# Layer-norm gains on GpSimd, an earlier decay step and halved first loads in a hybrid encoder kernel

## The chip, the cores and the metric

The kernel runs on one core of a Trainium2 chip. The metric is the device time of one execution in microseconds (us); smaller is better. The kernel before took 1337.24 us, the median of 3 runs between 1337.15 and 1337.52. The core has five engines that run their own instruction streams and meet at semaphores: TensorE (PE, matmuls), VectorE (DVE), ScalarE (ACT), GpSimd (POOL) and SyncE (SP, which here only issues DMAs).

## The reference

Two sequences of 256 tokens and 1024 channels pass through an initial layer norm and then two layers. One layer, cut to what matters:

```python
proj = h @ w_in                          # q, k, v, z, xbc, dt side by side
attn_out = window_attention(rope(q), rope(k), v, sink)      # |i-j| <= 128, 8 heads, 2 kv heads
xbc = silu(depthwise_conv(xbc, ssd_conv_w, ssd_conv_b))     # width 5
y = bidir_ssd(xs, dt_raw, dt_bias, a_log, bm, cm) + ssd_d * xs
ssd_out = rms_norm(y * silu(z), ssd_norm_g)
mix = concatenate([attn_out, ssd_out]) @ w_out
h = layer_norm(ALPHA * h + mix, ln1_g, ln1_b)
gate, val = split(h @ w_up)
ffn = (silu(depthwise_conv(gate, w, b)) * val) @ w_down     # width 3
h = layer_norm(ALPHA * h + ffn, ln2_g, ln2_b)
```

`layer_norm` is `(x - mean) * rsqrt(var + eps) * g + b`. All inputs and both outputs are float32.

## The kernel before, in words

All 512 tokens are worked on together, as 4 blocks of 128 tokens (t = 0 to 3) or as 8 tiles of 128 channels. Each weight matrix is cut into units of 128x1024 values: 105 units for a layer, numbered 0 to 104. Unit 0 is dt, 1 to 6 are k, v and four of q, 7 to 18 the convolved channels, 19 to 26 z, 27 to 38 the output projection, 39 to 82 the MLP's up projection, 83 to 104 the down projection.

Precision is kept by splitting: every weight unit `raw` is rounded by ScalarE to `whi` (L542), and VectorE forms `wlo = raw - whi` (L1118, "the split of a unit"). Activations are split in the same way into a high and a low part. Each product is then three matmuls: high by high, high by low and low by high. Raw, high and low units lie in a ring of 5 slots; SP loads a unit when the unit five places ahead has been used, and the split of unit n + 4 is written into the steps of unit n.

The order of the mixer is one list, `SCHED`, made by `mixer_schedule()` (L91). Every engine walks the same list and issues its own part of each step. The steps that the change touches or that stand near it:

- `G` n: the matmuls of unit n. `E` n: ScalarE copies the unit's result out of PSUM. For q and k these are four copies into the single tile `ropet` (the swapped halves, L648) and one into `qk` (L651); the four wait for the rotation before.
- `ROT`: the rotation, three VectorE operations (L1353, L1355, L1356). `S` n: the high and low part of weight unit n.
- `AA`, `AO`, `SM` (at unit 5): cumulative decays for the state-space part. TensorE sums them, ScalarE copies the high parts (`own_hi` L679, `off_hi` L684), VectorE makes from them `own_z`, `off_z`, `cum_a`, `own_w` and `off_w` (L1318 to L1338).
- `F`, `F2`: the taps of the convolution (L1254), from unit 7 on. `AS`, `AM`, `AX`, `AD`, `AN`, `AP`, `AV`: the attention of one block, from unit 8 on; `AN` is GpSimd's scaling (L505), `AP` TensorE's transposes (L1058).
- `RMS` and `RN` (in the output projection): the reciprocal (L1432), then for each of the 8 channel tiles a product with the gain (L1433, L1441) and the low part `alo` (L1445). `GN` (L1435): two operations of `gain` each, in units 31 to 34.

`gain` (L1121) multiplies by the layer norm's gain row and then adds its shift row, in token layout, for the residual path: in `ha` for the first norm of a layer and in `hb` for the second, 8 operations of 128x1024 each. `ha` is loaded back from DRAM (`h_kept`, L456), where `hb` has been stored; the gain and shift rows `gb` are a DMA of 1 MB (L435). The semaphore `affined` counts these operations; the sums of the next layer norm wait for it.

Unit 27 + k of the output projection has its k-th input tile in `ahi`, `alo`. Tiles 0 to 3 are attention, 4 to 11 the normalized state-space output, so unit 31 waits for the first low part and for its own weight split. TensorE does the first three units in banks 0 to 5 early, and comes back to their banks 6 and 7 (6 matmuls each) once the `std` of RMS is read.

After the last layer, block t is finished by: the sum with the matmul result (L1138, for t = 3 in halves L1494), the mean, the centred product with the gain `y1` (L1501), on ScalarE the squares and the root (L547, L549), the reciprocal (L1162), and two halves of `hb = y1 * rstd + shift` (L1508), each stored by its own DMA.

## Time and profile before

The profiled execution took 1337.52 us; its span, from the first instruction to the last, is 1335.7 us.

| | busy us | share of the span | instructions |
|---|---|---|---|
| PE (matmul) | 1313.1 | 98% | 6692 |
| DVE | 801.7 | 60% | 1076 |
| ACT | 581.0 | 43% | 883 |
| POOL | 103.8 | 8% | 71 |

TensorE's mean granted clock was 0.998. Times in the rows below are counted from the span's start. A row of the timeline gives the start, the time taken in us, the engine, the source line, the operation, what it writes and reads by the program's names, the shapes, how many equal instructions were merged (x2), and in brackets how long the engine was idle before and which engine ended that. For merged instructions the time is that of all together. On TensorE matmuls overlap, so the distance between their starts counts and not their own duration.

### The profile page before, as it was taken

The numbers are of one execution on the slowest core, as the hardware profiler recorded it, in microseconds if no ns is written. First come the engines' busy times: TensorE is split into PE (matmuls) and PEld (weight loads), VectorE is DVE, ScalarE is ACT, GpSimd is POOL, SyncE is SP. The second block draws the span as 40 slices with busy tenths as digits, with TensorE's granted clock in tenths as the row PEclk, the third lists the DMA queues.
The fourth block names the chain that finished last, engine by engine and source line by source line (L and its number), as shares of the span: only waits on it lengthen the run. The fifth ranks groups of instructions, "written<-read, shape, count | busy, mean of one in ns | idle before, by whom it ended". The sixth has DMA issues, their size and how long they took to land.

```text
span 1335.7 us, 16322 instructions
## 1 busy us (share of the span) xinstructions
PE 1313.1 (98%) x6692; PEld 1078.9 (81%) x6692; DVE 801.7 (60%) x1076; ACT 581.0 (43%) x883; POOL 103.8 (8%) x71
## 2 busy tenths in 40 slices
PE   8999999999999999999999999999999999999997
PEld 7877777788888888888888777787788888888885
DVE  6787888867444444442367878788564444443425
ACT  5756554436333333311266665544363333333112
POOL 2013500001000000000020234000010000000000
PEclk9999999999999999999999999999999999999999
DMA  5421121423332323333234211224223333223332
GB/s 189 151 79 49 61 66 49 173 79 97 100 103 95 95 95 95 128 101 100 67 101 157 64 49 63 64 88 149 94 81 102 102 95 95 95 95 127 99 103 97
DMA packets 33786, 129.94 MB, mean 97 GB/s; under 512 B 3792, under 2 KB 3952, under 8 KB 32560
## 3 DMA queue, kind: packets, MB, share of 16 engines
q1 hardware_dynamic: 33552, 128.61, 29.3%
q8 instruction: 53, 0.87, 0.3%
q0 software_dynamic: 160, 0.29, 0.1%
q14 instruction: 21, 0.17, 0.0%
HBM read 122.59 MB, written 6.29 MB: 96 GB/s over the span
## 4 chain that ended last, share of the span: by engine, by line
PE 79%; DVE 10%; ACT 7%; issue 2%; DMA 1%; POOL 0%; SPq 0%; DVEq 0%; ACTq 0%; POOLq 0%
PE ps L782 16%; PE ps L784 16%; PE ps L783 16%; PE ps L832 8%; PE ps L834 8%; PE ps L833 8%; PE ps L1027 2%; ACT ropet L648 1%; DVE wlo L1118 1%; DMA raw<-in_units 1%; ACT junk L547 1%; ACT sc L714 1%; DVE hb L1138 1%; ACT whi L542 1%; PE ps L824 1%
## 5 line engine op out<-in xcount | busy, mean ns | idle before, releaser
L782 PE MATMUL ps<-hhi,whi 128*128 128x512 f32 (+1 forms) x1200 | 457.7, 381 | 2.3 <-DVE hlo L1185 2.3
L783 PE MATMUL ps<-hlo,whi 128*128 128x512 f32 (+1 forms) x1200 | 453.6, 378 | 0.0
L784 PE MATMUL ps<-hhi,wlo 128*128 128x512 f32 (+1 forms) x1200 | 453.5, 378 | 0.0
L1118 DVE TENSOR_TENSOR wlo<-raw,whi 128x1024 fp32r<-128x1024 f32 x210 | 262.9, 1255 | 167.4 <-ACT whi L542 167.4
L542 ACT ACTIVATE whi<-raw 128x1024 fp32r<-128x1024 f32 x210 | 221.2, 1056 | 220.5 <-DMA raw<-in_units 220.5
L782 PEld LDWEIGHTS ps<-hhi,whi 128*128 128x128 f32 x1200 | 225.7, 188 | 45.8 <-issue 2.8
L784 PEld LDWEIGHTS ps<-hhi,wlo 128*128 128x128 f32 x1200 | 225.7, 188 | 42.2
L783 PEld LDWEIGHTS ps<-hlo,whi 128*128 128x128 f32 x1200 | 225.9, 188 | 41.5
L832 PE MATMUL ps<-whi,uhi 128*128 128x512 f32 x352 | 137.1, 390 | 0.0
L833 PE MATMUL ps<-whi,ulo 128*128 128x512 f32 x352 | 137.0, 389 | 0.0
L834 PE MATMUL ps<-wlo,uhi 128*128 128x512 f32 x352 | 136.9, 389 | 0.0
L1456 DVE SCALAR_TENSOR_TENSOR gcv<-ps,pf,gcv 128x510 f32<-128x510 f32 x44 | 33.0, 749 | 154.7 <-ACT gcv L752 154.6
L752 ACT ACTIVATE gcv<-ps,pf 128x512 f32<-128x512 f32 x44 | 34.4, 781 | 169.3 <-PE ps L784 169.3
L1466 DVE TENSOR_TENSOR guf<-gsg,ps 128x512 f32<-128x512 f32 x44 | 30.3, 688 | 82.9 <-PE ps L784 82.3
L832 PE MATMUL ps<-whi,ahi 128*128 128x512 f32 x192 | 75.7, 394 | 1.7 <-ACT std L738 1.7
L834 PEld LDWEIGHTS ps<-wlo,uhi 128*128 128x128 f32 x352 | 66.1, 188 | 13.7
L833 PEld LDWEIGHTS ps<-whi,ulo 128*128 128x128 f32 x352 | 66.1, 188 | 13.7
L832 PEld LDWEIGHTS ps<-whi,uhi 128*128 128x128 f32 x352 | 66.1, 188 | 13.6
L834 PE MATMUL ps<-wlo,ahi 128*128 128x512 f32 x192 | 74.8, 389 | 0.0
L833 PE MATMUL ps<-whi,alo 128*128 128x512 f32 x192 | 74.8, 389 | 0.0
L1254 DVE SCALAR_TENSOR_TENSOR cv<-ps,pm,cv 128x508 f32<-128x508 f32 (+1 forms) x96 | 71.4, 744 | 3.8 <-ACT cv L638 1.2
L484 POOL TENSOR_TENSOR hlo<-hfm,hhi 128x512 fp32r<-128x512 f32 x16 | 21.1, 1334 | 664.5 <-ACT hhi L574 664.5
(169 smaller groups left out, 1332.0 us busy)
## 6 DMA issues: line engine op xcount, KB each, us to landing
raw<-in_units SPq DMA_DIRECT2D x210, 512.0 KB, 3.5
gb<-in_gb SPq DMA_DIRECT2D x5, 1024.0 KB, 5.7
h_kept<-hb SPq DMA_DIRECT2D x2, 2048.0 KB, 9.1
ha<-h_kept SPq DMA_DIRECT2D x2, 2048.0 KB, 8.3
hb<-in_x SPq DMA_DIRECT2D x4, 512.0 KB, 6.4
out_y<-hb SPq DMA_DIRECT2D x8, 256.0 KB, 2.0
cn<-in_cn SPq DMA_DIRECT2D x1, 583.5 KB, 10.0
pm<-in_pm POOLq DMA_DIRECT2D x2, 80.0 KB, 3.4
```

The costliest lines, as they stand in the source:

```text
L542: A(whi[:, m % RING, :], raw[:, m % RING, :], ACT.Copy).then_inc(unit_hi, 1)
L752: A(gcv[:], ps[:, bank, :], ACT.Identity, scale=pf[:, k * 3 + w0 + 1:k * 3 + w0 + 2], bias=pf[:, k + v0:k + v0 + 1]).then_inc(glu_center, 1)
L782: mm(out, whi[:, slot, cols], xhi, start=start, stop=False)
L783: mm(out, whi[:, slot, cols], xlo, start=False, stop=False)
L784: return mm(out, wlo[:, slot, cols], xhi, start=False, stop=stop)
L832: mm(ps[:, bank, :], xhi[:, rows], whi[:, slot, cols], start=start, stop=False)
L833: mm(ps[:, bank, :], xlo[:, rows], whi[:, slot, cols], start=False, stop=False)
L834: return mm(ps[:, bank, :], xhi[:, rows], wlo[:, slot, cols], start=False, stop=stop)
L1118: V.tensor_tensor(wlo[:, m % RING, :], raw[:, m % RING, :], f(whi[:, m % RING, :]), ALU.subtract).then_inc(unit_split, 1)
L1254: V.scalar_tensor_tensor(out=dst[:, :, lo:hi], in0=src[:, :, lo + s:hi + s], scalar=pmc("conv_w", 5 * j + tap, 5 * j + tap + 1), in1=dst[: ...
L1456: V.scalar_tensor_tensor(out=dst[:, :, 1:SEQ], in0=src[:, :, 0:SEQ - 1], scalar=pf[:, k * 3 + w0:k * 3 + w0 + 1], in1=dst[:, :, 1:SEQ], op ...
L1466: V.tensor_tensor(guf[:], gsg[:], ps[:, bank + 1, :], ALU.mult).then_inc(glu_done, 1)
```

## The change

Five things are changed. (1) `AA`, `AO`, `SM` stand ahead of unit 5's rotation and weight split instead of behind them. (2) All `gain` operations go from VectorE to GpSimd, in a new function `affine` that does the four products and then the four additions. (3) The first two blocks of x are loaded in halves with a semaphore for each, and the statistics of the first half wait only for it. (4) For the last norm, `y1` has two buffers; for blocks 0 and 1, ScalarE multiplies by `rstd` and GpSimd adds the shift row, and one DMA stores each of these blocks. (5) The order of SP's last stores follows.

```diff
@@ mixer_schedule
+        if n == 5:
+            steps += [("AA", 0), ("AO", 0), ("SM", 0)]
         if n - 1 == U_V:
             steps += [("VT", 0)]
...
         steps += [("F", n)]
-        if n == 5:
-            steps += [("AA", 0), ("AO", 0), ("SM", 0)]
...
         steps.append(("S", u + AHEAD))
-        i = u - U_OUT - 4
-        if 0 <= i < NBLK:
-            steps += [("GN", 2 * i), ("GN", 2 * i + 1)]
@@ SP
             for t in range(2):
-                sp_eng.dma_start(hb[:, t, :], x_in[t]).then_inc(x_loaded[t], 16)
+                for half in range(2):
+                    cols = slice(half * 512, (half + 1) * 512)
+                    sp_eng.dma_start(hb[:, t, cols], x_in[t][:, cols]).then_inc((x_left if half == 0 else x_loaded)[t], 16)
...
-            for t in range(NBLK):
+            for t in range(2):
+                sp_eng.wait_ge(y_shifted, t + 1)
+                sp_eng.dma_start(y_d[t], hb[:, t, :]).then_inc(y_stored, 16)
+            for t in range(2, NBLK):
                 for half in range(2):
                     cols = slice(half * 512, (half + 1) * 512)
-                    sp_eng.wait_ge(y_ready, 2 * t + half + 1)
+                    sp_eng.wait_ge(y_ready, 2 * (t - 2) + half + 1)
                     sp_eng.dma_start(y_d[t][:, cols], hb[:, t, cols]).then_inc(y_stored, 16)
@@ GpSimd
+            def affine(idx, h):
+
+                pool.wait_ge(gb_loaded, idx * 16 + 16)
+                for t in range(NBLK):
+                    nc.gpsimd.tensor_tensor(h[:, t, :], h[:, t, :], gb[:, 0, :], ALU.mult).then_inc(affined, 1)
+                for t in range(NBLK):
+                    pool.wait_ge(affined, idx * 2 * NBLK + t + 1)
+                    nc.gpsimd.tensor_tensor(h[:, t, :], h[:, t, :], gb[:, 1, :], ALU.add).then_inc(affined, 1)
...
+                pool.wait_ge(h_loaded, L * 16 + 16)
+                affine(2 * L, ha)
                 lows(2 * L + 1)
+                pool.wait_ge(tp_full, (2 * L + 2) * NBLK)
+                affine(2 * L + 1, hb)
                 if L < DEPTH - 1:
                     lows(2 * L + 2)
+            pool.wait_ge(gb_loaded, (NORMS - 1) * 16 + 16)
+            for t in range(2):
+                pool.wait_ge(y_normed, t + 1)
+                nc.gpsimd.tensor_tensor(hb[:, t, :], hb[:, t, :], gb[:, 1, :], ALU.add).then_inc(y_shifted, 1)
@@ ScalarE
                     for t in range(NBLK):
-                        squares(2 * L + 2, t)
+                        squares(idx, t)
+                        if t < 2:
+                            act.wait_ge(ln_rstd, idx * NBLK + t + 1)
+                            act.wait_ge(y_scaled, t + 1)
+                            A(hb[:, t, :], y1[t][:], ACT.Copy, scale=st[:, t, 3:4]).then_inc(y_normed, 1)
@@ VectorE
-                dve.wait_ge(x_loaded[t], 16)
                 for half in range(2):
+                    dve.wait_ge((x_left if half == 0 and t < 2 else x_loaded)[t], 16)
...
-                    elif what == "GN":
-                        if i == 0:
-                            dve.wait_ge(h_loaded, L * 16 + 16)
-                        gain(2 * L, ha, i)
...
-                    if i == 0:
-                        dve.wait_ge(tp_full, (2 * L + 2) * NBLK)
-                    if 0 <= i < 2 * NBLK:
-                        gain(2 * L + 1, hb, i)
...
                     rstd(idx, t)
+                    if t < 2:
+                        continue
```

What this does to the order of the instructions, at three places. First, VectorE at units 4 to 6 of a layer, before (`ropet`, `qk` are a rotation, `wlo` a weight split, `own_z` to `off_w` the step SM):

```order
L1118 TENSOR_TENSOR wlo<-raw,whi 128x1024
L1353 TENSOR_TENSOR ropet<-ropet,cn 128x512
L1355 TENSOR_TENSOR qk<-qk,cn 128x512
L1356 TENSOR_TENSOR qk<-qk,ropet 128x512
L1118 TENSOR_TENSOR wlo<-raw,whi 128x1024
L1318 SCALAR_TENSOR_TENSOR own_z<-own_hi,cn,ps 128x512
L1324 SCALAR_TENSOR_TENSOR off_z<-off_hi,cn,ps 64x256 x2
L1328 TENSOR_SCALAR cum_a<-own_z,cn 128x512
L1330 TENSOR_SCALAR own_w<-own_z,cn 128x512 x2
L1338 TENSOR_SCALAR off_w<-off_z,cn 64x2x128 x4
L1353 TENSOR_TENSOR ropet<-ropet,cn 128x512
```

The same place now, from the split of unit 8 on (line numbers are those of the changed kernel):

```order
L1144 TENSOR_TENSOR wlo<-raw,whi 128x1024
L1335 SCALAR_TENSOR_TENSOR own_z<-own_hi,cn,ps 128x512
L1341 SCALAR_TENSOR_TENSOR off_z<-off_hi,cn,ps 64x256 x2
L1345 TENSOR_SCALAR cum_a<-own_z,cn 128x512
L1347 TENSOR_SCALAR own_w<-own_z,cn 128x512 x2
L1355 TENSOR_SCALAR off_w<-off_z,cn 64x2x128 x4
L1370 TENSOR_TENSOR ropet<-ropet,cn 128x512
L1372 TENSOR_TENSOR qk<-qk,cn 128x512
L1373 TENSOR_TENSOR qk<-qk,ropet 128x512
L1144 TENSOR_TENSOR wlo<-raw,whi 128x1024
L1370 TENSOR_TENSOR ropet<-ropet,cn 128x512
```

The five rows of SM have gone in front of one rotation and one weight split. Second, GpSimd from the last heads products to the next layer's start, before (`hlo` are low parts for the two layer norms, four each):

```order
L525 TENSOR_TENSOR heads_81<-cum_a,cn 128x1024
L514 TENSOR_TENSOR x_d_77<-xsc,pm 128x512 x3
L484 TENSOR_TENSOR hlo<-hfm,hhi 128x2x256 x8
L493 DMA pm<-in_pm 128x160
L494 DMA pf<-in_pf 128x120
```

The same place now:

```order
L538 TENSOR_TENSOR heads_81<-cum_a,cn 128x1024
L527 TENSOR_TENSOR x_d_77<-xsc,pm 128x512 x3
L495 TENSOR_TENSOR ha<-ha,gb 128x1024 x4
L498 TENSOR_TENSOR ha<-ha,gb 128x1024 x4
L488 TENSOR_TENSOR hlo<-hfm,hhi 128x2x256 x4
L495 TENSOR_TENSOR hb<-hb,gb 128x1024 x4
L498 TENSOR_TENSOR hb<-hb,gb 128x1024 x4
L488 TENSOR_TENSOR hlo<-hfm,hhi 128x2x256 x4
L506 DMA pm<-in_pm 128x160
L507 DMA pf<-in_pf 128x120
```

Eight operations on `ha` and eight on `hb` have come in, and each group of low parts stands behind one. Third, ScalarE at the end of the program, before (`junk` are the squares of one block):

```order
L547 ACTIVATE junk,st<-hb,st 128x1024
L549 ACTIVATE st<-st,cn 128x1
L547 ACTIVATE junk,st<-hb,st 128x1024
L549 ACTIVATE st<-st,cn 128x1
L547 ACTIVATE junk,st<-hb,st 128x1024
```

The same place now:

```order
L568 ACTIVATE junk,st<-hb,st 128x1024
L570 ACTIVATE st<-st,cn 128x1
L799 ACTIVATE hb<-y_0_97,st 128x1024
L568 ACTIVATE junk,st<-hb,st 128x1024
L570 ACTIVATE st<-st,cn 128x1
L799 ACTIVATE hb<-y_1_98,st 128x1024
L568 ACTIVATE junk,st<-hb,st 128x1024
```

A product with `rstd` stands behind the squares of blocks 0 and 1.

## Rows read from the trace of the kernel before

**Rows 1.** The page's first part: busy us (share) xinstructions of each engine.
```profile
PE 1313.1 (98%) x6692; PEld 1078.9 (81%) x6692; DVE 801.7 (60%) x1076; ACT 581.0 (43%) x883; POOL 103.8 (8%) x71
```
**Rows 2.** TensorE's waits: line, released by, us in total, times, longest us.
```profile
PE ps L824 <- DVE hb L1157: 2.4, 2, 1.3
```
**Rows 3.** Timeline of TensorE, 56 to 83 us.
```profile
56.99 0.50 PE L782 MATMUL ps<-hhi,whi 128*128 128x512 f32 x1
...
68.01 0.39 PE L782 MATMUL ps<-hhi,whi 128*128 128x512 f32 x1
...
73.45 0.39 PE L1042 MATMUL ps<-cut,big_i 128*128 128x256 f32 x2
...
82.16 1.09 PE L1058 MATMUL ps<-cn,sc 128*128 128x128 f32 x8 [0.28 <-POOL sc L505]
```
**Rows 4.** Timeline of ScalarE, the same stretch.
```profile
59.54 1.05 ACT L542 ACTIVATE whi<-raw 128x1024 fp32r<-128x1024 f32 x1
60.49 0.59 ACT L679 ACTIVATE own_hi<-ps 128x512 fp32r<-128x512 f32 x1
...
62.77 2.44 ACT L648 ACTIVATE ropet<-ps 32x512 f32<-32x512 f32 x4 [1.03 <-PE ps L784]
65.23 0.60 ACT L651 ACTIVATE qk<-ps 128x512 f32<-128x512 f32 x1
```
**Rows 5.** Timeline of VectorE, the same stretch.
```profile
62.25 0.74 DVE L1318 SCALAR_TENSOR_TENSOR own_z<-own_hi,cn,ps 128x512 fp32r<-128x512 f32 x1
...
66.85 0.69 DVE L1353 TENSOR_TENSOR ropet<-ropet,cn 128x512 f32<-128x512 f32 x1
...
70.16 3.16 DVE L1254 SCALAR_TENSOR_TENSOR cv<-ps,pm,cv 128x508 f32<-128x508 f32 x4
```
**Rows 6.** Timeline of GpSimd, 145 to 152 us.
```profile
145.28 4.21 POOL L525 TENSOR_TENSOR heads<-cum_a,cn 128x1024 fp32r<-128x1024 f32 x2
```
**Rows 7.** Timeline of VectorE, the same stretch.
```profile
145.84 1.89 DVE L1261 SCALAR_TENSOR_TENSOR xsc<-xsc,cv 128x512 f32<-128x512 f32 x1 [0.40 <-ACT xsc L669]
147.65 2.92 DVE L1118 TENSOR_TENSOR wlo<-raw,whi 128x1024 fp32r<-128x1024 f32 x1
```
**Rows 8.** The page's costliest groups: count, busy us, mean ns, idle before.
```profile
L484 POOL TENSOR_TENSOR hlo<-hfm,hhi 128x512 fp32r<-128x512 f32 x16 | 21.1, 1334 | 664.5 <-ACT hhi L574 664.5
```
**Rows 9.** Timeline of VectorE, 250 to 262 us.
```profile
251.27 3.35 DVE L1432 RECIPROCAL std<-std 128x512 f32<-128x512 f32 x1 [3.84 <-ACT std L738]
...
257.99 1.22 DVE L1118 TENSOR_TENSOR wlo<-raw,whi 128x1024 fp32r<-128x1024 f32 x1
```
**Rows 10.** Timeline of TensorE, the same stretch.
```profile
251.38 0.47 PE L832 MATMUL ps<-whi,ahi 128*128 128x512 f32 x1 [0.87 <-ACT std L738]
```
**Rows 11.** Timeline of SyncE's DMA queue, 240 to 262 us.
```profile
242.49 0.33 SPq L456 DMA_DIRECT2D ha<-h_kept  x1
```
**Rows 12.** Line L456, the loads of ha of both layers.
```profile
DMA to landing us min/median/max: 7.9/8.3/8.7
```
**Rows 13.** Timeline from 0 to 32 us, the warm-up matmuls.
```profile
1.00 6.25 PE L796 MATMUL ps<-avg 128*128 128x128 f32 x36 [1.00 <-POOL avg L487]
...
10.18 2.40 PE L796 MATMUL ps<-avg 128*128 128x128 f32 x20
```
**Rows 14.** Timeline of VectorE, 1314 to 1336 us.
```profile
1314.72 1.22 DVE L1138 SCALAR_TENSOR_TENSOR hb<-hb,ps 128x1024 f32<-128x1024 f32 x1 [9.14 <-PE ps L834]
...
1316.17 1.29 DVE L1501 SCALAR_TENSOR_TENSOR y<-hb,st,gb 128x1024 f32<-128x1024 f32 x1
...
1317.78 0.17 DVE L1162 RECIPROCAL st<-st 128x1 f32<-128x1 f32 x1 [0.32 <-ACT st L549]
...
1328.47 0.68 DVE L1494 SCALAR_TENSOR_TENSOR hb<-hb,ps 128x512 f32<-128x512 f32 x1
```
**Rows 15.** Timeline of TensorE, 1324 to 1336 us.
```profile
1326.47 0.39 PE L834 MATMUL ps<-wlo,uhi 128*128 128x512 f32 x1
```
**Rows 16.** The chain of waits, 0 to 14 us: start us, us, what.
```profile
2.12 6.65 DMA raw<-in_units
```

More of the change, by code:

```diff
@@ L268, in trunk @@
         junk = at("junk", 102, [P, D_MODEL])
-        y1 = at("y1", 88, [P, D_MODEL])
+        y1 = [at("y1_0", 88, [P, D_MODEL]), at("y1_1", -CT * TOK * 4 // KB, [P, D_MODEL], start=base_h)]
         std = at("std", 92, [P, TOK])
@@ L294, in trunk @@
         x_loaded = [sem(f"x_loaded{t}") for t in range(NBLK)]
+        x_left = [sem(f"x_left{t}") for t in range(2)]
         pm_loaded, pf_loaded = sem("pm_loaded"), sem("pf_loaded")
@@ L327, in trunk @@
         h_low, h_lows = sem("h_low"), sem("h_lows")
+        y_normed, y_shifted = sem("y_normed"), sem("y_shifted")
         glu_center, glu_taps, glu_silu = sem("glu_center"), sem("glu_taps"), sem("glu_silu")
@@ L468, in _ @@
             load_gb(NORMS - 1)
-            for t in range(NBLK):
+            for t in range(2):
+                sp_eng.wait_ge(y_shifted, t + 1)
+                sp_eng.dma_start(y_d[t], hb[:, t, :]).then_inc(y_stored, 16)
+            for t in range(2, NBLK):
                 for half in range(2):
                     cols = slice(half * 512, (half + 1) * 512)
-                    sp_eng.wait_ge(y_ready, 2 * t + half + 1)
+                    sp_eng.wait_ge(y_ready, 2 * (t - 2) + half + 1)
                     sp_eng.dma_start(y_d[t][:, cols], hb[:, t, cols]).then_inc(y_stored, 16)
-            sp_eng.wait_ge(y_stored, NBLK * 2 * 16)
+            sp_eng.wait_ge(y_stored, 6 * 16)
         @block.gpsimd
@@ L771, in _ @@
                 else:
+                    idx = 2 * L + 2
                     for t in range(NBLK):
-                        squares(2 * L + 2, t)
+                        squares(idx, t)
[3 more added lines that the diff above has]
+                            A(hb[:, t, :], y1[t][:], ACT.Copy, scale=st[:, t, 3:4]).then_inc(y_normed, 1)
         @block.tensor
@@ L1119, in split @@
                                     ALU.subtract).then_inc(unit_split, 1)
-            def gain(idx, h, i):
-                t, row = i % NBLK, i // NBLK
-                if i == 0:
-                    dve.wait_ge(gb_loaded, idx * 16 + 16)
-                if row:
-                    dve.wait_ge(affined, idx * 2 * NBLK + t + 1)
-                V.tensor_tensor(h[:, t, :], h[:, t, :], gb[:, row, :], ALU.add if row else ALU.mult).then_inc(affined, 1)
             def sums(idx, t, last_unit=0):
@@ L1474, in _ @@
                     split(unit(L, n + AHEAD))
-                    i = n - U_DOWN - 3
-                    if i == 0:
-                        dve.wait_ge(tp_full, (2 * L + 2) * NBLK)
-                    if 0 <= i < 2 * NBLK:
-                        gain(2 * L + 1, hb, i)
                 if L < DEPTH - 1:
@@ L1500, in _ @@
                     dve.wait_ge(ln_mu, (idx - 1) * NBLK + t + 1)
-                    V.scalar_tensor_tensor(out=y1[:], in0=hb[:, t, :], scalar=st[:, t, 1:2], in1=gb[:, 0, :],
+                    V.scalar_tensor_tensor(out=y1[t % 2][:], in0=hb[:, t, :], scalar=st[:, t, 1:2], in1=gb[:, 0, :],
                                            op0=ALU.add, op1=ALU.mult).then_inc(y_scaled, 1)
                     rstd(idx, t)
+                    if t < 2:
+                        continue
                     dve.wait_ge(ln_rstd, idx * NBLK + t + 1)
@@ L1507, in _ @@
                         cols = slice(half * 512, (half + 1) * 512)
-                        V.scalar_tensor_tensor(out=hb[:, t, cols], in0=y1[:, cols], scalar=st[:, t, 3:4], in1=gb[:, 1, cols],
+                        V.scalar_tensor_tensor(out=hb[:, t, cols], in0=y1[t % 2][:, cols], scalar=st[:, t, 3:4], in1=gb[:, 1, cols],
                                                op0=ALU.mult, op1=ALU.add).then_inc(y_ready, 1)
```

## The prediction

> **What bounds the kernel now.** I read the page's first part, then TensorE's waits, then the timeline of each engine where the change touches it. TensorE is busy for 98% of the span [rows 1]; its idle time is the start, the end and waits of about a microsecond, such as 2.4 us in two waits for the first normalized block [rows 2]. So work taken off VectorE in mid-kernel buys nothing unless TensorE waits for VectorE there, and a stall put on TensorE in mid-kernel comes back in full, for nothing later has room to absorb it. The questions are two: can the change shorten the ends, and does it make TensorE wait in the middle?
>
> **The block decay step moved ahead (SM at unit 5), in both layers.** TensorE's order stays; ScalarE and VectorE change. In the first layer unit 8's matmuls start at 68.01 and reuse the bank of unit 6, which ScalarE has copied out by 65.83 (65.23 + 0.60) [rows 3, 4]. After the change own_hi goes where the weight split stood, at 59.54, and ends at 60.1 [rows 4]. VectorE then runs SM, 66.85 - 62.25 = 4.6 us [rows 5], until 64.7, and only then the rotation of unit 5, three operations of 0.69, 2.1 us, until 66.8. ScalarE's copies of unit 6 wait for that rotation, because they write the one ropet tile: they take 2.44 + 0.60 [rows 4] and end at 69.9. TensorE's unit 8 so starts 1.9 us late. VectorE's next rotation waits for the swapped rows at 69.3, ends at 71.4, the split behind it (1.22 [rows 9]) at 72.6, and the convolution taps start at 72.7 instead of 70.16 [rows 5]: 2.5 us late. From there the chain taps, score maximum, exponentials, GpSimd scaling ends in the transposes at 82.16, where TensorE already waits 0.28 us for GpSimd [rows 3], so the whole 2.5 us arrive at TensorE (the 1.9 are inside them). Before, this ran under TensorE's matmuls because unit 6's copies overlapped SM; that cover is what the move takes away. Bounds: 1.9 if the chain has 0.6 us of slack that I don't see, 3.5 if ScalarE's table load falls badly. I take 2.5, twice: **+5.0 us**. The nearest ground for "nothing" would be slack at unit 8, but the copy ends only 2.2 us ahead of it and slips by 4.1.
>
> **The gains (GN and those in the down projection) moved from VectorE to GpSimd.** 16 operations per layer of 128x1024, both inputs in SBUF. GpSimd's price: its 128x512 subtraction with two SBUF inputs takes 1.33 us on average [rows 8], its broadcast product of 128x1024 takes 4.21 us for two, of which I show below that VectorE held up a part, so about 1.8 each [rows 6]. Bounds for one: 1.8 and 2 x 1.33 = 2.7; I take 2.5, near twice the dense one.
> The hb gains start when gb has landed in the down projection, where VectorE has nothing but one split per unit with three units in hand; eight take 20 us and nobody is waiting: 0.
> The ha gains are different. GpSimd starts when h_kept is back: issued at 242.49 [rows 11], landing 8.7 us later in this layer [rows 12], at 251.2. That is exactly when VectorE begins the reciprocal (251.27) and behind it, back to back, the norm products and low parts, all with two SBUF inputs, and the split of unit 31 at 257.99 [rows 9].
> What the trace shows of two such operations at once: GpSimd runs two heads products from 145.28, 4.21 us in all [rows 6]. VectorE's product xsc<-xsc,cv begins at 145.84 and lasts 1.89 us; the split behind it begins at 147.65 and lasts 2.92 us instead of 1.22 [rows 7, 9]. So the first waited for GpSimd's first product to end (147.1), then GpSimd's second went ahead of the split, which waited for 149.4. They take turns, and each waits for the other's whole instruction.
> The Trainium skill, "SBUF — State Buffer", section "Who interferes with whom", says the same of a VectorE instruction with two SBUF inputs against a GpSimd one that reads SBUF: the one that starts first blocks the other fully. It spares VectorE instructions with an input from PSUM, such as the taps; by that rule the loss sits in the norm stage and not in the convolutions. It says nothing of who is next, which I read from the turns above.
> Turn by turn: GpSimd's products 1 and 2 until 256.2; norm product 0 (due at 254.6); then one GpSimd operation ahead of each of product 1, low 0, product 2, low 1 and the split of unit 31. That makes 7 GpSimd operations and 5 VectorE ones of (257.99 - 254.62)/5 = 0.67, where 254.62 is the reciprocal's end, 251.27 + 3.35 [rows 9]: 251.2 + 7 x 2.5 + 5 x 0.67 + 1.2 = 273.3. TensorE needs that split for unit 31. It has 18 + 24 matmuls before it from 251.38 [rows 10], at (73.45 - 56.99)/72 = 0.229 each [rows 3]: 261.0. Stall: 12.3 us. The next split follows after the eighth GpSimd operation and four short ones, at 273.3 + 2.5 + 2.7 + 1.2 = 279.7, when TensorE has finished unit 31 at 278.8: 0.9 more. From there VectorE is alone and ahead again. Together 13.2 us. In the second layer the load takes 7.9 us [rows 12] and the same sum gives 0.9 less, 12.3. **+25.5 us.**
> A silent TensorE may come back slower. At the program's start, out of idleness, the warm-up matmuls take 6.25 us for 36 passes; ten microseconds later the same take 2.40 us for 20 [rows 13]. At the later pace of 0.12 the first ones would have taken 4.3, so they lost 1.9 us. The mean granted clock of the run is 0.998, so no fall in mid-kernel is shown. Per stall that is between 0 and 1.9 us, and 0.9 of it hides in the second wait; I take the slow start at its full size less that, 1.0 each, **+2.0 us**.
> The Trainium skill, "TensorE: Matmul & The Clock Gate", section "Why this matters for your kernels", warns of such gaps in the middle of a kernel: the clock falls to 1.2 GHz. No run here shows it yet; without it the sum is 2.0 less.
>
> **The end.** VectorE paces it: TensorE's last matmul starts at 1326.47 [rows 15], and VectorE gets to block 3 only at 1328.47 [rows 14], since each block costs it (1328.47 - 1314.72)/3 = 4.58 us against TensorE's 18 matmuls, 4.1. A block's y product starts 1.45 us after its sum. Blocks 0 and 1 lose their last VectorE step, some 1.4 us (two halves of the y product's kind, 1.29 for the whole). Alone that lets VectorE start block 2 at 1322.9 when it is ready, and block 3 at 1327.5: -1.0. But GpSimd's additions (hb and gb, 2.5 us) get in the way of the y products (hb and gb too). Block 0: reciprocal at 1317.78, ScalarE's product 1.1 (its rounding of the same shape takes 1.05 [rows 4]), addition 1319.1 to 1321.6. Block 1 is ready at 1318.8, its y is due at 1320.25 and waits to 1321.6, ends at 1322.9; its addition runs 1324.2 to 1326.7; block 2's y is due at 1324.55, waits to 1326.7, and the rest of block 2 ends at 1329.55. Block 3 starts there: **+1.1 us**. Bounds -1.0 and +1.3.
>
> **The start.** The chain is the load of unit 0 (issued 2.12, landed 8.77) and then ScalarE's rounding and VectorE's split [rows 16]. The x blocks arrive before that; halves give a sooner first statistic that nobody waits for. Two more issues on the queue put unit 0's issue 0.9 us back, but the engines are still full with x then. Between 0 and +0.9; I take **+0.2**.
>
> **Sum.** 5.0 + 25.5 + 2.0 + 1.1 + 0.2 = 33.8 on the profiled execution's 1337.5: 1371.3. That execution lies 0.3 above the median, so 1371.0 us.
>
> **Rivals.**
> 1. VectorE keeps the ports once it has them, and GpSimd gets in only where VectorE pauses. Then norm product 0 waits 1.5 us and the split of unit 31 is ready at 260.7, just ahead of TensorE. For it: only two turns of this kind are in the trace, one per layer. Against it: in both GpSimd's second product went ahead of a waiting split. It gives 1337.2 + 5.0 + 1.1 + 0.2 = 1343.5.
> 2. Turns are taken, but GpSimd loses every second one (its dispatch is slow against 0.67 us steps), or its operation costs 1.8. With 5 instead of 7 the stall is 5 us shorter in each layer: about 1359. With 1.8 us it is 7 x 0.7 = 4.9 shorter: the same 1359. Nothing in the trace speaks for the first; the row of 4.21 us for two speaks a little for the second.
> 3. The other side: faster. VectorE's inputs in the norm stage and the end don't collide with GpSimd's, and SM's move has slack. Place: the end, -1.0 us, deciding from the point where GpSimd's additions no longer hold the y products. 1336.2. Against it are the two stretched rows of VectorE [rows 7].
> 4. The change has no effect at all because TensorE never waits for what moved: 1337.
>
> **Chances.** Forecast (full turns) 0.65; rival 2, 0.16; rival 1, 0.13; rival 3 and 4 together 0.06. The forecast's own range: GpSimd's operation at 2.3 to 2.7 (-2.8 to +2.8 over both layers), clock 0 to 1.9 each, SM 1.9 to 3.5, ends: 1364 to 1379. The range for 8 in 10 reaches to rival 2: 1355 to 1380. A measurement of this kernel tells 0.2% (2.7 us) from no change. Faster by more than that 0.02, within it 0.04, slower 0.94.
>
> **What would show it.** In the profile after: VectorE's norm products, low parts and the split of unit 31 each lengthened to about 3 us just after the reciprocal, alternating with GpSimd's eight gains; TensorE idle for 11 to 13 us in front of unit 31 in both layers, put down to the split; the first matmuls behind it perhaps at twice their spacing. In units 6 to 9, a wait of about 2 us in front of unit 8 for ScalarE's qk copy. At the end, the y products of blocks 1 and 2 at about 2.6 us or more, and block 3 begun about 3 us after TensorE's last matmul. The prediction is wrong if the splits in the norm stage keep 1.2 us, or if TensorE doesn't stop before unit 31.

## The result, and the profile after

The changed kernel takes 1368.19 us in the median of 4 runs (1366.8 to 1370.16), the kernel before 1337.2 us on the same chip: ratio 1.0232, 95% interval 1.0215 to 1.025. The forecast was 1371.0. The profiled execution's span grew by 31.3 us, from 1335.7 to 1367.0, while TensorE's instructions stayed 6692 and VectorE's fell by 36.

TensorE's waits in the profile after (total, number, longest):

```profile
PE ps L858 <- DVE wlo L1144: 18.8, 2, 9.9
PE ps L850 <- DVE hb L1174: 3.0, 2, 1.7
PE ps L808 <- ACT qk L672: 2.2, 2, 1.9
```

The first row is new: two waits for a weight split. The second was already there [rows 2]; the third is the wait ahead of unit 8. To see where 31.3 us arose I compared the start of the same TensorE instruction in both traces:

| place | before | after | shift |
|---|---|---|---|
| first matmul of unit 0 | 13.67 | 14.20 | +0.5 |
| first attention block, layer 1 | 73.45 | 77.79 | +4.3 |
| after the convolutions | 110.70 | 114.24 | +3.5 |
| end of layer 1's mixer | 299.73 | 315.69 | +16.0 |
| small matmuls of the decays, layer 2 | 699.68 | 717.52 | +17.8 |
| first transposes, layer 2 | 739.11 | 757.89 | +18.8 |
| end of layer 2's mixer | 956.72 | 987.48 | +30.8 |
| VectorE's block 3 at the end | 1328.47 | 1359.78 | +31.3 |

So there are two steps of 12.4 and 12.0 us, one in each layer's norm stage; 3.0 and 2.8 us in the early units; and half a microsecond each at the start and at the end. In layer 2, 1.7 of the 2.8 us arise before unit 8, where TensorE ran at half clock for some 3 us behind a wait that stands in the kernel before too (1.05 us here, 0.99 before, where the clock held). The last section comes back to this.

VectorE in the norm stage of layer 1, after (start, duration, operation, idle time before):

```profile
254.86 3.35 DVE L1449 RECIPROCAL std<-std 128x512 f32<-128x512 f32 x1 [3.84 <-ACT std L759]
258.25 2.01 DVE L1450 SCALAR_TENSOR_TENSOR zs<-zs,pm,std 128x512 f32<-128x512 f32 x1
260.18 2.88 DVE L1454 SCALAR_TENSOR_TENSOR zs<-zs,pm,std 128x512 f32<-128x512 f32 x1
...
268.54 2.83 DVE L1458 TENSOR_TENSOR alo<-zs,ahi 128x512 fp32r<-128x512 f32 x1
271.29 3.36 DVE L1144 TENSOR_TENSOR wlo<-raw,whi 128x1024 fp32r<-128x1024 f32 x1
274.57 2.85 DVE L1454 SCALAR_TENSOR_TENSOR zs<-zs,pm,std 128x512 f32<-128x512 f32 x1
277.34 0.68 DVE L1458 TENSOR_TENSOR alo<-zs,ahi 128x512 fp32r<-128x512 f32 x1
```

GpSimd beside it:

```profile
254.96 10.36 POOL L495 TENSOR_TENSOR ha<-ha,gb 128x1024 f32<-128x1024 f32 x4 [79.62 <-DMA ha<-h_kept]
265.27 11.59 POOL L498 TENSOR_TENSOR ha<-ha,gb 128x1024 f32<-128x1024 f32 x4
```

And TensorE, where a matmul follows the last by 0.227 us at full clock:

```profile
264.38 0.39 PE L860 MATMUL ps<-wlo,ahi 128*128 128x512 f32 x1
274.70 0.80 PE L858 MATMUL ps<-whi,ahi 128*128 128x512 f32 x1 [9.93 <-DVE wlo L1144]
275.29 0.63 PE L859 MATMUL ps<-whi,alo 128*128 128x512 f32 x1
...
279.13 0.44 PE L859 MATMUL ps<-whi,alo 128*128 128x512 f32 x1
279.42 0.39 PE L860 MATMUL ps<-wlo,ahi 128*128 128x512 f32 x1
```

Before, the reciprocal was followed by steps of 0.67 us and the split of unit 31 at 257.99 [rows 9]. Now every step of VectorE from the second product on grows by about 2.13 us for as long as GpSimd has gains to run (until 276.86), and falls back to 0.68 at once afterwards. The first product meets GpSimd in the middle of an instruction and grows by 1.26. The split is ready at 274.65, and TensorE goes on at 274.70. The reciprocal keeps its 3.35 us, although GpSimd runs beside it. Behind the wait the matmuls start 0.43 us apart until 279.1, half the normal pace; the granted clock of these stretches:

```profile
274.00:276.00 2.00, 1.30 (x3) 1.11 (x4) 2.00 (x2) 0.00 (x0) 2.00 (x1) 0.50 0.00 0
...
280.00:282.00 2.00, 2.00 (x11) 1.63 (x10) 2.00 (x4) 0.88 (x2) 0.00 (x0) 1.00 0.00 0
```

The third number from the right is the clock: 0.50 (1.2 GHz), later 1.00 (2.4 GHz). Layer 2 shows the same, with a wait of 8.82 us and slow matmuls from 945.76 to 951.5.

### The profile page after: what moved, and what is told of

Read it like the earlier page. It is cut to its first block, busy times and chain, and to the rows that moved or that the text cites. A ratio compares the mean times of both kernels' runs of the same rounds, so it can differ in the third digit from the quotient of the medians.

```text
span 1367.0 us, 16323 instructions
## 1 busy us (share of the span) xinstructions
PE 1322.9 (97%) x6692; PEld 1084.7 (79%) x6692; DVE 800.5 (59%) x1040; ACT 583.5 (43%) x885; POOL 197.1 (14%) x105
## 4 chain that ended last, share of the span: by engine, by line
PE 79%; DVE 11%; ACT 7%; issue 1%; DMA 1%; POOL 0%; SPq 0%; DVEq 0%; ACTq 0%; POOLq 0%
PE ps L808 16%; PE ps L809 16%; PE ps L810 16%; PE ps L858 7%; PE ps L859 7%; PE ps L860 7%; PE ps L1053 2%; ACT ropet L669 1%; DVE wlo L1144 1%; ACT sc L735 1%; PE ps L850 1%; DVE hb L1155 1%; ACT junk L568 1%; DVE ast L1419 1%; DMA raw<-in_units 1%
## 5 line engine op out<-in xcount | busy, mean ns | idle before, releaser
L1144 DVE TENSOR_TENSOR wlo<-raw,whi 128x1024 fp32r<-128x1024 f32 x210 | 274.1, 1309 | 193.9 <-ACT whi L563 193.9
L858 PE MATMUL ps<-whi,ahi 128*128 128x512 f32 x192 | 78.3, 408 | 20.5 <-DVE wlo L1144 18.8
L495 POOL TENSOR_TENSOR hb<-hb,gb 128x1024 f32<-128x1024 f32 x8 | 22.0, 2776 | 498.2 <-DMA gb<-in_gb 498.2
```

The source lines that it names most:

```text
L858: mm(ps[:, bank, :], xhi[:, rows], whi[:, slot, cols], start=start, stop=False)
L1144: V.tensor_tensor(wlo[:, m % RING, :], raw[:, m % RING, :], f(whi[:, m % RING, :]), ALU.subtract).then_inc(unit_split, 1)
```

## The experiments

Each of the moved parts alone, then changed in the way that separates two causes. "Before" was run beside each; its median lay between 1337.4 and 1337.9.

### The ha gains alone

```
-        if 0 <= i < NBLK:
-            steps += [("GN", 2 * i), ("GN", 2 * i + 1)]
+                pool.wait_ge(h_loaded, L * 16 + 16)
+                affine(2 * L, ha)          # GpSimd, ahead of lows
```

> Only the gains and shifts of ha are moved to GpSimd; everything else is the kernel before. Theory (turns: while GpSimd has a two-input operation to run, each of VectorE's operations of 0.67 us waits for GpSimd's whole one and the next waits again, 2.8 us a pair): the split of unit 31 is ready at about 273.3 to 274.7 instead of before TensorE needs it at 261, in both layers, so 24 us longer: 1361.5 (1359 to 1363.5), with VectorE's rows at 2.8 us in both norm stages and TensorE idle 9 to 10 us on that split. Rival (the move of these operations costs little and the time comes from the moved decay step and the tail together with it): at most 1341. Rival (VectorE goes at its own pace and is only delayed once by 2.5): 1341 to 1343.

Measured: 1361.2 us in the median of 4 runs, ratio 1.0171 (1.0152 to 1.019). One of the four took 2670 us, for a reason that no trace shows; the others took 1360.0 to 1361.7, median 1360.65, which is +23.3. VectorE's steps take 2.87 and 2.88 us there, and

```profile
PE ps L840 <- DVE wlo L1126: 18.8, 2, 9.9
```

is the same row as in the whole change. This one part makes 23 to 24 of the 31 us. In its trace 0.9 of the 24.2 us that it is longer come from half clock at the start of layer 2.

### The same gains, a few microseconds later

```
                 pool.wait_ge(h_loaded, L * 16 + 16)
+                pool.wait_ge(sl_done, L * CT + CT)
                 affine(2 * L, ha)
```

> As the one with only the ha gains on GpSimd, but GpSimd also waits until VectorE has made the last of the eight low parts of the normalized output, so the same sixteen... (eight) operations run a few us later, beside a TensorE that has its weights split ahead. Theory turns: what costs is only that the operations meet the one stretch in which VectorE is late for TensorE; here VectorE has slack of several us, so the same operations cost 0 to 2 us: 1337.2 (1336.5 to 1339.5), though VectorE's operations beside them are still stretched to 2.8 us in the rows. Rival (GpSimd's operations cost TensorE's time by themselves, by memory traffic, or the whole stage waits for ha): it stays at 1355 or above.

Measured: 1337.86 us (10 runs), ratio 1.0004 (0.9995 to 1.0013). The collision is still in the trace, VectorE first, then GpSimd:

```profile
268.35 16.72 DVE L1127 TENSOR_TENSOR wlo<-raw,whi 128x1024 fp32r<-128x1024 f32 x5 [0.25 <-ACT whi L551]
```

```profile
268.23 12.43 POOL L488 TENSOR_TENSOR ha<-ha,gb 128x1024 f32<-128x1024 f32 x4 [96.98 <-DVE alo L1454]
```

Five splits take 16.72 us, 3.34 each instead of 1.22, but TensorE spends 24 matmuls of 0.227, 5.4 us, on a unit and has no wait between 267 and 290 us. The same eight operations per layer cost 23 to 24 us or, within the interval, at most 1.7, depending on whether TensorE is waiting for VectorE's work when they run. A cost of that size by GpSimd or its memory traffic as such is ruled out.

### The gains in halves

```
-                    nc.gpsimd.tensor_tensor(h[:, t, :], h[:, t, :], gb[:, 0, :], ALU.mult)
+                        for half in range(2):
+                            cols = slice(half * 512, (half + 1) * 512)
+                            ins = nc.gpsimd.tensor_tensor(h[:, t, cols], h[:, t, cols], gb[:, row, cols], ...)
```

> As the one with only the ha gains on GpSimd, but as 16 operations of 128x512 per layer instead of 8 of 128x1024. Theory turns (VectorE waits for one whole instruction of GpSimd before each of its own): each of VectorE's operations in the norm stage is stretched by about 1.1 to 1.3 instead of 2.13 us (rows of 1.8 to 2.0 for those that take 0.68 to 0.75), the eight rows ahead of TensorE's need end at about 265.5 instead of 273.3, so TensorE's first wait is 2 to 3 us instead of 9.9 and then further ones come while GpSimd still runs: each unit then needs one split and four operations, (1.22 + 4 x 0.72 + 5 x 1.2) = 10 against 3.6 us of TensorE, so the rest of the delay comes back as later waits: in all 18 to 24 us over both layers, 1355 to 1361. Rival (the total of GpSimd's busy time beside VectorE decides, as a shared bandwidth): each operation stretched by a fixed factor of about 4 as before, first wait unchanged at 9.9, 1361. Rival (shorter instructions let VectorE pass): 1345 or less.

Measured: 1354.84 us (1354.2 to 1355.7), ratio 1.0125 (1.0111 to 1.0139), just below my range. VectorE in the norm stage:

```profile
257.58 1.78 DVE L1457 TENSOR_TENSOR alo<-zs,ahi 128x512 fp32r<-128x512 f32 x1
259.29 1.77 DVE L1453 SCALAR_TENSOR_TENSOR zs<-zs,pm,std 128x512 f32<-128x512 f32 x1
260.98 1.75 DVE L1457 TENSOR_TENSOR alo<-zs,ahi 128x512 fp32r<-128x512 f32 x1
262.66 2.28 DVE L1130 TENSOR_TENSOR wlo<-raw,whi 128x1024 fp32r<-128x1024 f32 x1
```

With GpSimd's instruction half as long, what is added to each VectorE step is half as long: 1.77 - 0.72 = 1.05 us instead of 2.13. A shared bandwidth would have left the factor of 4 alone. TensorE's waits in front of unit 31 and the two units behind it are 3.66, 0.39 and 1.09 us in layer 1 (I had expected 2 to 3 for the first), and 4.10 and 1.67 in layer 2. The work gets through sooner although GpSimd does the same amount: per turn VectorE does a step for 1.05 us of GpSimd and not for 2.13.

### GpSimd only writes

```
+                for n in range(40):
+                    nc.gpsimd.memset(scratch[:], 0.0).then_inc(filled, 1)
+                    pool.wait_ge(filled, L * 40 + n + 1)
```

> The kernel before, with 40 memsets of 128x512 on GpSimd beside the norm stage of each layer, at the time at which the moved ha gains would run; they write to an unused piece of SBUF and nothing reads it. What the two engines contend for: theory A (the path by which both read two operands, so a GpSimd instruction that only writes doesn't hold VectorE): VectorE's rows stay 0.68 and 0.75, 1337.4 (1336.8 to 1338). Theory B (any GpSimd instruction that touches SBUF takes its turn with VectorE): rows of VectorE grow by the length of one memset (0.3 to 0.6 us) each, TensorE waits for the split of unit 31 a few us or not at all, 1338 to 1350.

Measured: 1337.4 us (10 runs), ratio 0.9998 (0.9989 to 1.0007). GpSimd, then VectorE inside that stretch:

```profile
250.43 23.36 POOL L533 MEMSET scratch<- 128x512 f32 x40 [79.17 <-DMA ha<-h_kept]
```

```profile
256.90 0.68 DVE L1451 TENSOR_TENSOR alo<-zs,ahi 128x512 fp32r<-128x512 f32 x1
257.50 1.22 DVE L1124 TENSOR_TENSOR wlo<-raw,whi 128x1024 fp32r<-128x1024 f32 x1
```

Forty memsets back to back leave VectorE's rows where they were. So GpSimd's writing to SBUF doesn't hold VectorE. By elimination what collides is its reading of operands (theory A); a GpSimd instruction that reads only one was not tried, so this step is argued and not shown. The other half of the condition stands in the changed kernel's own trace, in an attention block: VectorE's taps read one operand from PSUM, and beside GpSimd's two-operand scaling

```profile
83.51 1.52 DVE L1271 SCALAR_TENSOR_TENSOR cv<-ps,pm,cv 128x510 f32<-128x510 f32 x2
```

```profile
83.74 1.89 POOL L518 TENSOR_TENSOR sc<-sc,ast 128x1024 f32<-128x1024 f32 x1 [54.02 <-DVE ast L1430]
```

neither is stretched: the two taps take 1.52 us, as the pair at 81.04 does (1.53) with GpSimd idle. The scaling takes 1.89, its mean over all 16.

### The hb gains alone

```
+                pool.wait_ge(tp_full, (2 * L + 2) * NBLK)
+                affine(2 * L + 1, hb)      # GpSimd; VectorE's gain() calls go
```

> Only the gains and shifts of hb are moved to GpSimd, which runs them beside VectorE's splits of the down projection. Theory turns: VectorE's splits beside them go from 1.22 to 3.35 us, which is less than the 3.63 us that TensorE takes for a unit, and they are made units ahead, so TensorE never waits for one: 1337.4 (1337.0 to 1338.2). Rival (any meeting of the two engines costs TensorE time in proportion to the overlap, 2 x 8 x 2.1 us): 1350 or more. Rival (VectorE is relieved of 16 operations of 1.2 us and the end of the layer comes earlier): 1336.5 or less.

Measured: 1337.63 us (11 runs), ratio 0.9998 (0.9989 to 1.0006). No cost is seen, and one above 0.8 us is ruled out. The splits beside the gains take 1.65 to 2.63 us, less than I expected, since VectorE idles over 3 us before each and meets only part of a GpSimd instruction. (A unit is 24 matmuls, 5.4 us, and not the 3.63 of the expectation; that makes the slack larger.)

### The decay step alone

```
+        if n == 5:
+            steps += [("AA", 0), ("AO", 0), ("SM", 0)]     # ahead of the splits
         ...
-        if n == 5:
-            steps += [("AA", 0), ("AO", 0), ("SM", 0)]     # was behind F
```

> Only the step of the decay sums (AA, AO, SM at unit 5) is moved ahead of the splits. Theory: in each layer ScalarE copies ropet and qk 1.9 us late, unit 8 and the first attention block start 1.9 to 2.5 us late, and in layer 1 the wait of 1.9 us is followed by some 3 us at half clock (1.6 us more). From the two traces: +3.0 in layer 1 and +0.9 in layer 2, so 1341.2 (1339.5 to 1343). Rival of the prediction as written (2.5 in each layer, reaching the transposes, plus the clock): 1342.2 to 1344. Rival (the step costs nothing by itself and the 3 us are an after-effect of the later start): 1337.2 to 1338.

Measured: 1342.83 us (1342.4 to 1343.3), ratio 1.004 (1.0026 to 1.0054), +5.4. The wait ahead of unit 8, and the matmuls behind it:

```profile
69.67 0.50 PE L782 MATMUL ps<-hhi,whi 128*128 128x512 f32 x1 [1.89 <-ACT qk L651]
70.02 0.55 PE L783 MATMUL ps<-hlo,whi 128*128 128x512 f32 x1
...
73.35 0.48 PE L782 MATMUL ps<-hhi,whi 128*128 128x512 f32 x1
73.66 0.39 PE L783 MATMUL ps<-hlo,whi 128*128 128x512 f32 x1
```

Behind a wait of 1.9 us come 3 us at half pace (a later run shows the same wait without them). My account (3.0 in layer 1 because of the clock, 0.9 in layer 2) came to 1.5 us too little; the time lies in the range of the prediction as written. Layer 2 cost 2.7: its first 1.7 are a fall of the clock at its start, which the 1.0 of the later stage only tops up. That asks whether the clock is a cost at all, and the next two runs test it.

### Matmuls without use in front of unit 8, and then also at the start of layer 2

```
                         if i == 8:
+                            keep_warm(8, 5)
...
                     elif what == "DTT":
+                        if L:
+                            keep_warm(4, 5)       # second of the two kernels only
```

> The moved decay step alone, and eight matmuls without use (0.24 us each) on TensorE just ahead of its wait for unit 8, in both layers. Theory (the 1.9 us wait itself remains, but the 1.6 us that the half clock takes behind it in layer 1 goes): 1342.8 - 1.6 = 1341.2 (1340.4 to 1342), PEclk 1.00 from 66 to 78 us. In layer 2 the wait there is only 0.3 us, so the eight matmuls (1.9 us) would hold unit 8 up by some 1.6 us unless the next stage has slack: then 1342.8 and the gain of layer 1 is eaten. Rival (the clock falls for another reason than the wait): the same rows of 0.63 us at 70 to 74 us, 1342.8 or more.

> As the kernel with the moved decay step and the matmuls before unit 8, and four more matmuls without use (1.0 us) ahead of TensorE's wait for the copy of zt at the start of layer 2 (a wait of 1.0 to 1.15 us in every run, behind which the clock fell in five profiles and not in five others). Theory (filling that wait keeps the clock whole, 1.65 us in a profile that had the fall): 1.0 to 1.7 us less than the kernel with only the first eight matmuls, PEclk 1.00 from 688 to 700 us. Rival (the fall there is not brought on by the wait): no difference between the two, within 0.3 us.

Measured: 1342.73 us (1342.4 to 1343.0) and 1342.43 us (1342.3 to 1342.7). Both are within 0.4 of the decay step alone: my expectation of 1.6 less, and of another 1.0 to 1.7 less, failed. (The 1342.8 that I gave for a second outcome was met, but not for its reason: in layer 2 the eight matmuls did put unit 8 back, by 1.4 us, and at the end of the convolutions only 0.2 of it was left.) Yet the clock did what I asked. From 70 to 74 us, first the decay step alone, then with the eight matmuls:

```profile
70.00:74.00 4.00, 4.00 (x12) 3.15 (x11) 3.79 (x6) 3.46 (x4) 0.00 (x0) 0.57 0.16 65
```

```profile
70.00:74.00 4.00, 3.95 (x17) 3.30 (x18) 3.87 (x6) 3.84 (x4) 0.00 (x0) 1.00 0.18 74
```

The clock is 1.00 instead of 0.57, and the first attention block starts at 75.60 instead of 76.87. It buys next to nothing, because TensorE then stands in front of the first transposes:

```profile
84.70 1.09 PE L1060 MATMUL ps<-cn,sc 128*128 128x128 f32 x8 [0.68 <-POOL sc L505]
```

Before that wait was 0.28 [rows 3]; in the decay step alone it is gone in this layer, and so is a later one of 0.60 for `alo`. The late chain through ScalarE, VectorE and GpSimd sets these places, and whether TensorE comes to them early or late matters little. Counted from unit 0, the layer ends 2.6 us late with the clock held and 3.0 without: the fall of 1.6 us costs 0.4. At the start of layer 2 it is the same. In the second of the two kernels the clock holds there (1.00 from 690 to 694, against 0.65 in the first), layer 2's first stage is 1.7 us shorter, and the wait at the transposes (743.99, 0.67 us for GpSimd) is still there: the decay step now costs 2.65 in that layer instead of 1.0.

### The halved loads of x alone

```
-                sp_eng.dma_start(hb[:, t, :], x_in[t]).then_inc(x_loaded[t], 16)
+                for half in range(2):
+                    cols = slice(half * 512, (half + 1) * 512)
+                    sp_eng.dma_start(hb[:, t, cols], x_in[t][:, cols])...
```

> Only the loads of the first two blocks of x are made in halves (four DMAs of 256 KB instead of two of 512 KB). Theory (the second half of block 1 lands last, at 7.5 us instead of the whole block before it, and the statistics of block 1 and so the first unit start 0.5 us later): first unit's matmuls at 14.2 instead of 13.7, 1337.9 (1337.4 to 1338.6). Rival of the prediction (two more issues of 0.05 us each, +0.2): 1337.4 to 1337.6. Rival (the first half is there earlier and the start gains): 1336.8 or less.

Measured: 1338.52 us (11 runs) against 1337.9, ratio 1.0003 (0.9994 to 1.0012): too small for the times. The trace has unit 0 at 14.38 instead of 13.67, +0.7. Unit 0 starts at 13.14 to 13.82 in the eleven profiles with whole loads and at 14.00, 14.20 and 14.38 in the three with halves, so some 0.7 us are lost there. In the changed kernel the chain to unit 0 runs through block 1 of x:

```profile
6.55 0.69 DVE L1166 BATCH_NORM_STATS2 moms<-hb 128x6 f32<-128x512 f32 x1 [1.37 <-DMA hb<-in_x]
7.56 0.69 DVE L1166 BATCH_NORM_STATS2 moms<-hb 128x6 f32<-128x512 f32 x1 [0.31 <-DMA hb<-in_x]
```

The statistics of block 1 wait for its second half, and its transposes end at 11.45. With the loads alone changed, the chain that sets unit 0 runs through its load, as before (start, us, what):

```profile
3.06 6.42 DMA raw<-in_units
```

It is issued at 3.06 instead of 2.12, because each of the two further issues takes 0.42 us with 0.05 between them (the expectation counts the 0.05 alone), and lands at 9.48 instead of 8.77: 0.71 later, what unit 0 loses. The two chains lie within 0.3 us of each other in both traces. The profile is 1.5 us longer in all; 0.9 of it are half clock at the start of layer 2, behind a wait of 1.07 us.

### The end alone

```
+                        if t < 2:
+                            A(hb[:, t, :], y1[t][:], ACT.Copy, scale=st[:, t, 3:4]).then_inc(y_normed, 1)
...
+            for t in range(2):
+                pool.wait_ge(y_normed, t + 1)
+                nc.gpsimd.tensor_tensor(hb[:, t, :], hb[:, t, :], gb[:, 1, :], ALU.add).then_inc(y_shifted, 1)
```

> Only the end is changed: for blocks 0 and 1 the last operation of the final layer norm goes to ScalarE (scaling) and GpSimd (shift). Theory (the two y operations of VectorE at the end wait for GpSimd's shift, 1.3 to 2.6 and 3.3 us, which eats what two fewer pairs of VectorE operations save): +0.5 against before, 1337.7 (1337.2 to 1338.3). Rival (VectorE is freed of 2 x 1.3 us and the end comes earlier): 1336.2. Rival (a second cost, ScalarE's reading of y1, comes on top): 1339 or more.

Measured: 1338.06 us (11 runs), ratio 1.0005 (0.9996 to 1.0014). The gain of 1 us is ruled out; +0.7 or nothing can't be told apart. In the trace two `y` products wait for GpSimd's addition:

```profile
1319.57 2.56 DVE L1514 SCALAR_TENSOR_TENSOR y<-hb,st,gb 128x1024 f32<-128x1024 f32 x1
...
1323.65 3.30 DVE L1514 SCALAR_TENSOR_TENSOR y<-hb,st,gb 128x1024 f32<-128x1024 f32 x1
```

They took 1.28 before. The 3.3 us given away eat up the two pairs of VectorE operations saved, 2 x 1.42. VectorE comes to block 3 2.54 us after TensorE's last matmul starts (1325.85), and 2.00 us in the kernel before: +0.5.

### The whole change, with the ha gains late

The edit is the one line of the second experiment, put into the changed kernel.

> The changed kernel with one thing more: GpSimd waits for the last of the eight low parts of the normalized output before the ha gains. Theory (the sum of the parts measured alone: decay step +5.4, x loads +0.6, hb 0, end +0.7, ha late +0.5): 1337.4 + 7.2 = 1344.6 (1343 to 1346.5), so the whole of the other 24 us is the meeting of the ha gains with the norm stage. Rival (parts that cost nothing alone cost something together, such as the hb gains against a VectorE that is already late): 1348 or more. Rival (the gains of the other parts show only now): 1341 or less.

Measured: 1344.87 us (1344.7 to 1345.0), ratio 1.0052 (1.0036 to 1.0067). One wait takes 23.3 of the 31 us back, and the parts add up: 1337.4 + 5.4 + 0.6 + 0 + 0.7 + 0.5 = 1344.6 (the last four terms are each too small to be told from nothing by themselves). The trace shows one thing more, in layer 1 in front of unit 8:

```profile
70.41 0.50 PE L809 MATMUL ps<-hhi,whi 128*128 128x512 f32 x1 [1.91 <-ACT qk L673]
70.75 0.40 PE L810 MATMUL ps<-hlo,whi 128*128 128x512 f32 x1
70.98 0.39 PE L811 MATMUL ps<-hhi,wlo 128*128 128x512 f32 x1
```

The same wait of 1.91 us as in the changed kernel, and the clock holds (1.00 from 70 to 76). Behind the wait of 1.92 us in layer 2 (730.24) it falls. Counted from unit 0, layer 1's early units cost 2.6 us here, as with the matmuls without use.

### The end in another order, on the kernel before

```
                     y1[t % 2] = (hb - mean) * gain        # block t
+                    if t:
+                        shifted(t - 1, 1)                  # second half of block t - 1
                     rstd(idx, t)
                     ...
                     shifted(t, 0)
```

> The kernel before with another order of VectorE's work at the very end: the second half of block t-1's last operation stands behind the centred product of block t, so that it fills the wait for the root on ScalarE. Theory (each of the three blocks before the last then hides one operation of about 0.75 us, but only the last blocks' queue counts, since VectorE waits for TensorE's block 3): -0.8 us, 1336.6 (1336.2 to 1337.1). Rival (VectorE waits for block 3's matmuls at the end anyway, so the order before them is worth nothing): 1337.4, within 0.3.

Measured: 1336.34 us (11 runs), ratio 0.9988 (0.9979 to 0.9996): faster than the kernel before, by 1.6 in the medians and 1.2 in the spans, where I had expected 0.8. VectorE:

```profile
1320.07 1.28 DVE L1507 SCALAR_TENSOR_TENSOR y<-hb,st,gb 128x1024 f32<-128x1024 f32 x1
1321.27 0.75 DVE L1488 SCALAR_TENSOR_TENSOR hb<-y,st,gb 128x512 f32<-128x512 f32 x1
1321.93 0.16 DVE L1162 RECIPROCAL st<-st 128x1 f32<-128x1 f32 x1
...
1326.97 0.68 DVE L1500 SCALAR_TENSOR_TENSOR hb<-hb,ps 128x512 f32<-128x512 f32 x1
```

The wait of 0.32 us for the root [rows 14] is filled in blocks 1, 2 and 3, and block 3 starts at 1326.97 instead of 1328.47. Moving VectorE's work within VectorE got what moving it to GpSimd did not.

## Why the prediction was right

**The turns (forecast +25.5).** The mechanism is as read from [rows 6, 7, 9]: seven GpSimd instructions run before VectorE's split of unit 31 does, and one stands ahead of every VectorE step. The whole-instruction wait was tested (halves) and holds: a turn is one whole GpSimd instruction and the VectorE step behind it. That writing alone doesn't collide (memsets) and that an operand from PSUM spares VectorE (taps) are in the traces. The size was off: a GpSimd gain adds 2.13 us to a turn, where I took 2.5 from the nearest rows. That is outside my range of 2.3 to 2.7, and a little nearer to the 1.8 of rival 2 than to my 2.5. Seven times 0.37 is 2.6 us per layer, and TensorE's waits are 9.9 and 8.8 instead of 12.3 and 11.4. The second wait of 0.9 did not come, since TensorE was slow just then. Waits together: 18.8 against 25.5. The Trainium skill, "SBUF — State Buffer", section "Who interferes with whom", spares a VectorE instruction with an operand from PSUM; the taps agree, at 0.76 us each beside GpSimd. That the engines alternate, instruction by instruction, is read from the row of every turn.

**The slow clock behind the waits (forecast +2.0).** This was too small. The step at layer 1 is 12.4 - 9.9 = 2.5 us beyond the wait, at layer 2 12.0 - 8.8 = 3.2: together 5.7, of which the half pace makes 2.2 and 2.9. I had read the loss from the program's start, 1.9 us at most [rows 13]; in mid-kernel 4.4 and 5.7 us went at half pace. The Trainium skill, "TensorE: Matmul & The Clock Gate", section "Why this matters for your kernels", warned of such gaps, and the trace agrees (0.50 behind both). The two errors work against each other: 27.5 forecast, 24.4 measured. That the total came within 3 us of the forecast owes something to this luck: with the 2.0 us of slow clock that I had forecast the change would have cost some 27 us (an estimate, 31.0 - 5.7 + 2.0).

**The decay step (forecast +5.0).** Right: +5.4 alone. TensorE's wait ahead of unit 8 (1.91 us in the trace, 1.9 forecast) and the late chain that ends in the transposes (2.6 us where the clock held, 2.5 forecast) were the terms. I did not think that the clock would fall behind 1.9 us; that it hardly mattered, the two kernels with added matmuls show.

**The hb gains (forecast 0).** Right, at 1337.63 against 1337.9 for the kernel before.

**The end (forecast +1.1).** Block 3 in the changed kernel starts 31.3 late where TensorE was 30.8 late: +0.5. The `y` products of 2.6 and 3.3 us are as drawn up; what I missed is that a `y` product held up gives ScalarE time to have the root ready, so that the wait of 0.32 us behind it [rows 14] goes; GpSimd's addition also took 2.41 and not 2.5.

**The start (forecast +0.2).** Too small. I had unit 0's load as the last to come, issued 0.9 us later, and took 0.2 of it. With the loads alone changed that chain does set the start, 0.7 us later. In the changed kernel the second half of block 1, which I had ahead of it, comes last, and unit 0 starts 0.5 us later. Both are within the bound of 0.9.

**The rivals.** VectorE keeping the ports (1343.5), every second turn lost (1359), a gain at the end (1336.2), no effect (1337): the turn period of 2.75 to 2.81 us for every product and low part, without one left out, excludes the first two, the end alone excludes the third, and the wait of 9.9 us for the split the last.

## What to carry to other kernels

Before moving an elementwise operation from VectorE to GpSimd, look at what VectorE runs at that moment: if both read two operands from SBUF, as here, each VectorE instruction waits for one whole GpSimd instruction. The price is then (number of VectorE steps on the critical stretch) times (length of a GpSimd instruction). If it must go to GpSimd, put it behind the stretch in which TensorE is waiting for VectorE, and if that can't be done, cut it into shorter instructions (6.4 us less here). And price a wait of TensorE by following it to the next place where it waits anyway: 10 us in mid-kernel came back in full and with interest, 1.6 us of slow clock ahead of such a place cost 0.4.

## What was not expected of the hardware

- Behind a wait of 1.9 us TensorE went at half pace for 3 us in three cases (1.89, 1.91, 1.92) and kept its clock in a fourth (1.91). At the start of layer 2 a wait of 1.0 to 1.2 us stands in every profile but the one where matmuls fill it. Behind it the clock fell in six of them (waits of 1.05, 1.07, 1.08, 1.15, 1.15, 1.20 us) and held in seven (0.99, 1.02, 1.07, 1.08, 1.08, 1.11, 1.17). The length of the wait does not decide; what does stays open. A fall there is worth 1.7 us at once and 0.9 after the next places where TensorE waits, in the kernel with only the x loads changed; some of the spread between runs of one kernel may come from this, which was not tested.
- GpSimd's gain takes 2.41 us (its addition at the end) and adds 2.13 to a VectorE step in a turn; 40 memsets of 128x512 take 23.36 us, 0.58 each, without lengthening VectorE's rows.
- VectorE's reciprocal, with one operand, runs through GpSimd's gains unchanged at 3.35 us.
